# The last expert's rows by a product with gated lists, and a reordered start, in a two-layer decoder kernel

## The reference

```python
h = x                                                  # 512 tokens x 1024
h = h + gla_mixer(rms_norm(h, a_norm), w_in, w_gk2, b_gk2, o_norm, w_out)
h = h + hier_moe(rms_norm(h, m_norm[0]), ...)
k, v = split(rms_norm(h, kv_norm) @ w_kv)
h = h + stick_breaking(rms_norm(h, b_norm) @ w_q, k, v) @ w_out
h = h + hier_moe(rms_norm(h, m_norm[1]), ...)
return rms_norm(h, final_norm)

def hier_moe(t):       # top-1 of 4 groups, top-2 of its 4 experts: 2 of 16 experts per token
    combine = weights of the two chosen experts, 0 elsewhere            # 512 x 16
    for e in range(16):
        hdn = silu(t @ w_gate[e]) * (t @ w_up[e])                       # 1024 -> 512
        y += combine[:, e:e+1] * (hdn @ w_down[e])                      # 512 -> 1024
```

## Time and profile before

| | us |
|---|---|
| three runs: median (lowest, highest) | 1307.45 (1304.81, 1307.50) |
| profiled execution, whole | 1304.74 |
| its span, first to last instruction | 1303.1 |
| PE busy | 1136.8 (87%) |
| DVE busy | 819.4 (63%) |
| ACT busy | 694.4 (53%) |
| POOL busy | 157.1 (12%) |
| PE in the chain that ended last | 77% |

### The profile page before, as it was taken

How to read it: one execution, slowest core, us unless ns; L and a number is a source line. 1 busy time by engine, 2 the same in 40 slices (tenths; PEclk the granted TensorE clock), 3 DMA queues, 4 the chain that set the end, 5 groups by cost and what they waited for, 6 DMA issues and landing times.

```text
span 1303.1 us, 14486 instructions
## 1 busy us (share of the span) xinstructions
PE 1136.8 (87%) x5477; PEld 859.9 (66%) x5477; DVE 819.4 (63%) x825; ACT 694.4 (53%) x732; POOL 157.1 (12%) x169
## 2 busy tenths in 40 slices
PE   5799997974999999995799989999839999999970
PEld 4488875853677777774578867767626777777740
DVE  2454236266888888885523346662568888888846
ACT  2442433243777777775233226662427777777742
POOL 1100030012010100001100004430030010010004
PEclk9899998985999999998799988999859999999995
DMA  8343103207999999996412210003069999999925
GB/s 282 79 145 130 33 1 117 77 17 235 385 391 393 403 392 392 403 371 243 147 65 98 97 33 1 1 17 129 1 222 374 394 399 390 393 394 411 380 75 193
DMA packets 89060, 283.49 MB, mean 218 GB/s; under 512 B 11704, under 2 KB 11872, under 8 KB 89008
## 3 DMA queue, kind: packets, MB, share of 16 engines
q1 hardware_dynamic: 70272, 239.09, 48.5%
q0 software_dynamic: 11024, 39.07, 9.0%
q10 hardware_dynamic: 7712, 4.63, 1.1%
HBM read 259.96 MB, written 22.81 MB: 217 GB/s over the span
## 4 chain that ended last, share of the span: by engine, by line
PE 77%; DVE 7%; issue 5%; POOL 4%; ACT 3%; DMA 2%; ACTq 1%; POOLq 0%; DVEq 0%
PE ps L1274 23%; PE ps L1276 23%; PE ps L1275 23%; PE ps L1458 2%; PE ps L1292 1%; POOL xn_r L1829 1%; DMA xn<-output_table,pos 1%; PE ps L1419 1%; DVE h L1170 1%; PE ps L1486 1%; DVE raw L1214 1%; DVE xn_r L1218 1%; DMA pad<-normed_rows,token 1%; POOL xn_r L1824 1%; POOL pad_r L1824 1%
## 5 line engine op out<-in xcount | busy, mean ns | idle before, releaser
L816 DVE TENSOR_TENSOR w_lo<-raw,w_hi 128x2048 fp32r<-128x2048 f32 x72 | 164.7, 2289 | 94.8 <-ACT w_hi L470 94.6
L470 ACT CAST w_hi<-raw 128x2048 fp32r<-128x2048 f32 x72 | 137.7, 1912 | 117.7 <-PE ps L1276 117.5
L1274 PE MATMUL ps<-xT_hi,s_hi 128*96 128x512 f32 (+1 forms) x392 | 157.0, 400 | 8.6 <-DVE s_lo L910 5.2
L816 DVE TENSOR_TENSOR xT_lo<-raw,xT_hi 128x2048 fp32r<-128x2048 f32 x64 | 146.1, 2288 | 20.4 <-ACT xT_hi L470 20.4
L1274 PE MATMUL ps<-w_hi,s_hi 128*96 128x512 f32 x384 | 154.7, 403 | 4.6 <-DVE s_lo L992 4.6
L1276 PE MATMUL ps<-xT_hi,s_lo 128*96 128x512 f32 (+1 forms) x392 | 155.5, 397 | 0.0
L1275 PE MATMUL ps<-xT_lo,s_hi 128*96 128x512 f32 (+1 forms) x392 | 154.7, 395 | 0.0
L1276 PE MATMUL ps<-w_hi,s_lo 128*96 128x512 f32 x384 | 152.9, 398 | 0.0
L1275 PE MATMUL ps<-w_lo,s_hi 128*96 128x512 f32 x384 | 152.1, 396 | 0.0
L470 ACT CAST xT_hi<-raw 128x2048 fp32r<-128x2048 f32 x64 | 122.0, 1912 | 38.3 <-PE ps L1276 38.3
L1274 PE MATMUL ps<-w_hi,xT_hi 128*128 128x512 f32 x304 | 122.1, 401 | 12.9 <-DVE w_lo L820 6.4
(11 more groups left out here) (282 smaller groups left out, 2004.9 us busy)
## 6 DMA issues: line engine op xcount, KB each, us to landing
raw<-in_m_w_up SPq DMA_DIRECT2D x64, 1024.0 KB, 10.5
xn<-in_m_w_gate SPq DMA_DIRECT2D x60, 1024.0 KB, 11.6
raw<-in_m_w_down SPq DMA_DIRECT2D x60, 1024.0 KB, 11.2
raw<-in_a_w_in SPq DMA_DIRECT2D x12, 1024.0 KB, 5.9
output_table<-pad POOLq DMA_DIRECT2D x32, 384.0 KB, 6.4
raw<-in_w_kv SPq DMA_DIRECT2D x8, 1024.0 KB, 7.4
raw<-in_a_w_out SPq DMA_DIRECT2D x4, 1024.0 KB, 5.7
raw<-in_m_w_gate SPq DMA_DIRECT2D x4, 1024.0 KB, 8.8
```

Source lines behind the costliest of these rows:

```text
L470: se.copy(hi, raw_block).then_inc(A["hi_done"], 1)
L816: ve.tensor_tensor(lo, raw_block, hi, ALU.subtract).then_inc(V["lo_done"], 1)
L1274: te.matmul(o, a_hi, b_hi, start=start, stop=False)
```

## The change

1. **The last expert of a layer** (expert 15) is not stored; the gathers read zeros for its rows. After the router's weights DVE makes gated lists in three more instructions: it multiplies `at_row` by the weight where the chosen expert is 15 (L1172 and L1173 of the changed kernel) and adds the halves of the two choices (L1174). PE transposes them into PSUM (L1543) after expert 1's input, and DVE copies them out to `last_rows`. After the last `y_out`, PE multiplies `last_rows` with `y_sb` (L1599, float32, two instructions of 512 columns for each token tile), and DVE adds the product to `h` from PSUM (L1188). Those are three additions for each tile instead of two. The table rows of expert 15 are zeroed at the start of the program.
2. **The overflow loop** stands ahead of the last down product on every engine. POOL's eight gathers now wait only for the first 15 stores.
3. **The additions' order** is changed (`ADDS`), and in layer 0 the tiles 1 to 3 are transposed only when all additions are done. `dense_first` makes the products of tiles 2 and 3 after the first transposition. The row of token factors moves from ahead of the last tile to between its two halves.
4. **The start**: tile 0 is transposed ahead of the gains. The low-rank weight and its three companions are loaded by SP after the input tiles, and they are scaled and split ahead of `tile_lo` of tiles 1 to 3. The squares stand between the tiles' copies. Panels are renumbered, so that the first one after the gates writes other PSUM banks than the gates' and need not wait for the bias.
5. **Smaller moves**: in the linear attention the score products stand ahead of the key transposes. Ahead of the stick-breaking attention, `panel_out_features(13)` stands ahead of `split(B + 13)`. In the last norm DVE does tiles 0, 1 and 3 in one step each, and POOL and ACT only tile 2.

```diff
+        ADDS = [(0, 0), (0, 1), (1, 0), (1, 1), (2, 0), (2, 1), (0, 2), (1, 2), (3, 0), (3, 1), (2, 2), (3, 2)]
+
+        def added(layer, i, k):
+
+            return len(ADDS) * layer + ADDS.index((i, k)) + 1
+
+        def last_banks(i):
+
+            first = (0, 3072, 1024, 3072)[i]
+            return psf[:, first:first + D]
...
                     load(streams[0][1], 1)
+            with nc.allow_non_contiguous_dma(reason="512 gate biases and 16 columns a row"):
+                for dst, src in ((lr_raw[:, :, :], a_w_in[0, :, GK0:GK0 + RANK].rearrange("(k p) r -> p k r", p=P)),
+                                 (wgk2, a_w_gk2[0]), (bgk[:, :], a_b_gk2[0].rearrange("(h p) -> p h", p=P)),
+                                 (onorm, a_o_norm[0].partition_broadcast(P))):
+                    sp.dma_start(dst, src).then_inc(A["small_loaded"], 16)
...
             LN_EXP = "natural_log_exp_and_others"
             se.preload_act_table_set(LN_EXP)
+            tile_hi(0, 0)
             act.wait_ge(V["gains_out"], 1)
-            tile_hi(0, 0)
             split(0)
             split(1)
+            act.wait_ge(V["lr_scaled"], 1)
+            se.copy(lr_hi, lr_raw[:, :, :]).then_inc(A["lr_hi_done"], 1)
             for i in range(1, NT):
                 tile_hi(0, i)
-            norm_squares(0)
-            act.wait_ge(V["lr_scaled"], 1)
-            se.copy(lr_hi, lr_raw[:, :, :]).then_inc(A["lr_hi_done"], 1)
+                squares_of(0, i - 1)
+            squares_of(0, NT - 1)
+            rsqrt_first(0, NT)
...
                 step(I + NE - 1, B + LAST, 0, False)
-                if layer + 1 < LAYERS:
-                    split((layer + 1) * L_BLOCKS)
-                    split((layer + 1) * L_BLOCKS + 1)
-                act.wait_ge(M["blk_used"], B + NE * E_BLOCKS)
-                y_out(E, I + NE - 1)
...
                 over_loop(act, layer, tile)
+                if layer + 1 < LAYERS:
+                    split((layer + 1) * L_BLOCKS)
+                    split((layer + 1) * L_BLOCKS + 1)
+                act.wait_ge(M["blk_used"], B + NE * E_BLOCKS)
+                act.wait_ge(G["over_ended"], layer + 1)
+                y_out(E, I + NE - 1)
...
+            tile_lo(0, 0)
             dve.wait_ge(M["gains_tr"], 1)
             ve.tensor_copy(gainT[:, :], ps[:, 7, 0:5 * KT]).then_inc(V["gains_out"], 1)
             dve.wait_ge(V["gains_out"], 1)
-            tile_lo(0, 0)
             split(0)
             split(1)
-            for i in range(1, NT):
-                tile_lo(0, i)
             dve.wait_ge(A["small_loaded"], 16 * SMALL)
             ve.tensor_tensor(lr_raw[:, :, :], lr_raw[:, :, :], gainT[:, 0:KT].unsqueeze(2).broadcast_to([P, KT, RANK]),
                              ALU.mult).then_inc(V["lr_scaled"], 1)
+            dve.wait_ge(A["lr_hi_done"], 1)
+            ve.tensor_tensor(lr_lo, lr_raw[:, :, :], lr_hi, ALU.subtract).then_inc(V["lr_lo_done"], 1)
+            for i in range(1, NT):
+                tile_lo(0, i)
             norm_scale(0)
             diagonals()
...
                 over_loop(dve, layer, tile)
+                if layer + 1 < LAYERS:
+                    split((layer + 1) * L_BLOCKS)
+                    split((layer + 1) * L_BLOCKS + 1)
...
                 link(tt(w12[:, 1, :], w12[:, 0, :], ex, ALU.mult))
-
-            def combine(layer, first=0, last=2 * NT):
-
-                for n in range(first, last):
-                    i, k = COMBINE[n]
+                link(stt(base_k, tile_k, float(NE - 1), w12[:, :, :].rearrange("p k i -> p (k i)"), ALU.is_equal, ALU.mult))
+                link(tt(at_row, at_row, base_k.unsqueeze(2).broadcast_to([P, 2 * NT, CAP]), ALU.mult))
+                tt(at_row[:, 0:NT, :], at_row[:, 0:NT, :], at_row[:, NT:2 * NT, :], ALU.add).then_inc(V["last_ready"], 1)
...
+            def combine(layer, first, last):
+
+                for i, k in ADDS[first:last]:
                     if k == 0:
-                        dve.wait_ge(gathered[i], 32 * (layer + 1))
-                    if k:
-                        dve.wait_ge(V["combined"], 2 * NT * layer + n)
-                    ve.scalar_tensor_tensor(h[:, i, :], y_rows[n], w12[:, k, i:i + 1], h[:, i, :],
-                                            ALU.mult, ALU.add).then_inc(V["combined"], 1)
+                        dve.wait_ge(E[f"x_loaded{i}"], 16 * GATHERS * (layer + 1))
+                    else:
+                        dve.wait_ge(V["combined"], added(layer, i, k - 1))
+                    if k < 2:
+                        ins = ve.scalar_tensor_tensor(h[:, i, :], y_rows[COMBINE.index((i, k))], w12[:, k, i:i + 1], h[:, i, :],
+                                                      ALU.mult, ALU.add)
+                    else:
+                        dve.wait_ge(M["last_done"], NT * layer + i + 1)
+                        ins = ve.tensor_tensor(h[:, i, :], h[:, i, :], last_banks(i), ALU.add)
+                    ins.then_inc(V["combined"], 1)
...
             split(B + 2)
-            for i in range(NT):
-                combine(0, 2 * i, 2 * i + 2)
-                if i:
-                    tile_lo(3, i - 1)
-            tile_lo(3, NT - 1)
+            combine(0, 0, 8)
+            tile_lo(3, 0)
+            combine(0, 8, 12)
+            for i in range(1, NT):
+                tile_lo(3, i)
...
             split(B + 12)
+            panel_out_features(13, B + 11, qT1[:, 4:8, :], SD ** -0.5)
             split(B + 13)
-            panel_out_features(13, B + 11, qT1[:, 4:8, :], SD ** -0.5)
...
             experts(1)
-            combine(1, 0, 5)
+            combine(1, 0, 8)
             mean_square(4, 0, 2)
-            combine(1, 5, 6)
+            combine(1, 8, 11)
             refine(0, 2, final=1)
-            combine(1, 6, 8)
+            combine(1, 11, 12)
+            normed(2, [0, 1])
             mean_square(4, 2, NT)
             refine(2, NT, final=2)
...
                     half(j, 0)
                     if j < NT - 1:
                         transposed_tile(turn, event, j + 1)
+                    else:
+                        between_half()
                     half(j, 1)
...
-            dense_first(0, 0, 0, 0, low_rank)
+            dense_first(0, 0, 0, 0, gains_transposed, low_rank, token_factors)
             pe.wait_ge(V["lr_out"], 1)
             for i in range(GH):
                 ins = te.matmul(ps[:, 4 + i, :], wgk2[:, DK * i:DK * (i + 1)], lrT, start=True, stop=True)
             ins.then_inc(M["gates_done"], 1)
+            pe.wait_ge(A["panel_out"], 1)
+            dense(2, 2, True)
             pe.wait_ge(V["gates_in"], GH)
-            dense(1, 2, True)
-            pe.wait_ge(A["panel_out"], 1)
-            dense(2, 4, True)
+            dense(3, 4, True)
...
+            pe.wait_ge(V["k_toend"], 1)
+            pe.wait_ge(A["panel_out"], 4)
...
                 x_transposed(E, I + 1, 1, first_load)
+                pe.wait_ge(V["last_ready"], layer + 1)
+                for t in range(NT):
+                    ins = te.transpose(ps[0:CAP, 7, P * t:P * (t + 1)], at_row[:, t, :], ident[:, :])
+                ins.then_inc(M["last_tr"], 1)
...
                 h_transposed(E, i)
-                down(i, c + 6)
...
                 over_loop(pe, layer, tile)
+                down(i, c + 6)
+
+            def last_to_tokens(layer, tiles):
+
+                pe.wait_ge(V["last_out"], layer + 1)
+                pe.wait_ge(E["y_out"], NE * (layer + 1))
+                for i in tiles:
+                    if i == 3:
+                        pe.wait_ge(V["combined"], added(layer, 1, 2))
+                    for n in range(2):
+                        ins = te.matmul(last_banks(i)[:, BN * n:BN * (n + 1)], last_rows[:, P * i:P * (i + 1)],
+                                        y_sb[:, BN * n:BN * (n + 1)], start=True, stop=True)
+                    ins.then_inc(M["last_done"], 1)
...
-            dense_first(8, B, 3, 2, lambda: rstd_row_sums(2))
+            last_to_tokens(0, (0, 1))
+            dense_first(8, B, 3, 2, lambda: last_to_tokens(0, (2, 3)), lambda: None, lambda: rstd_row_sums(2))
...
             experts(1)
+            last_to_tokens(1, range(NT))
...
-                for i in range(1, NE + 1):
+                for i in range(1, NE):
                     if i + XG + 1 < NE:
                         gather_next(i + XG + 1)
                     pool.wait_ge(E["y_out"], I + i)
                     store(E, (i - 1) * CAP)
-                pool.wait_ge(E["y_stored"], 16 * (I + NE))
+                pool.wait_ge(E["y_stored"], 16 * (NE - 1) * (layer + 1))
+                pool.wait_ge(V["lo_done"], blocks_of(layer) + NE * E_BLOCKS)
+                pool.wait_ge(G["zeroed"], 16 * (MAX_OVER + 1))
                 S = O[layer]
...
             pool.wait_ge(G["gain_loaded"], 16 * 3)
-            for i in range(NT - 1):
-                wait_h(pool, 4, i)
```

(3 more changed lines are left out.)

133 lines of the change are left out of this document (63 added, 70 removed).

## The result

| us | before | changed |
|---|---|---|
| median of the runs | 1306.27 (4 runs, 1304.81 to 1307.50) | 1287.14 (4 runs, 1283.90 to 1287.73) |
| ratio, 95% interval | | 0.985 (0.983 to 0.987) |
| span of the profiled execution | 1303.1 | 1285.6 |
| granted clock, mean | 0.936 | 0.947 |

The account below looks back on a forecast made before the run. PE was taken as the bound, through its idle time and clock. Terms -14.6, 0, +3.3, -2.8, -1.9 and -5.3 sum to -21.3, from 1304.7 to 1283.4 us, said as 1284; forecast's own range 1279 to 1289, 8 in 10 for 1277 to 1292.

Parts of the forecast that it names:

- Term 1: Start of the kernel: earlier first matmul, no waits for the low-rank weight or gates' bias, fewer slow matmuls; -14.6 us.
- term 2: Linear attention: score products ahead of key transposes gain nothing, since both orders end at ACT; 0, bounds -1 to +1 us.
- the two old delays: Small loads at the start: taking turns with large weight descriptors (-14.6 us), or 16.2 us from issue to landing (-12.2).
- no wait over 1 us: Sign of being right: PE has no such wait between the first matmul, near 14.8, and 170 us.
- All at 2.4 GHz from about 19: Sign of being right: PE keeps its higher clock from about 19 us up to 170 us.
- Term 3: Router: three more DVE instructions ahead of the experts' first splits delay PE 1.65 us in each of two layers; +3.3 us.
- Term 4: End of layer 0's experts: gathers start 9.2 us sooner, most of it given back by additions and products; -2.8 us.
- six gathered additions and one from PSUM: End of layer 0's experts: these DVE additions (1.28 us each, and 1.2) bring tile 0 to 624.3 us.
- rival (a): Ends of both layers: third addition and float32 products use up the detour's gain, terms 4 and 6 are 0; 1291.5 us, chance 0.13.
- rival (d): Last down product: the loop's branch stalls PE, up to 2 us a layer; 1287.4 us, chance 0.05.
- Term 5: Ahead of the stick-breaking attention: L883 starts at the panel's end with the split behind it, 1.9 us sooner; -1.9 us.
- Term 6: End of the program: gathers 7.9 us sooner, 2.6 lost to DVE's longer chain; -5.3 us, bounds -7.9 to -1.

Follow-up runs that it names:

- experiment 3: Changed kernel with the four small loads issued by ACT behind the gains again, not by SP; median 1292.06 us, ratio 0.990 to the kernel before.
- Experiment 2: Changed kernel with DVE's three factor instructions moved from the router to behind the first expert's `x_lo`; median 1284.00 us, ratio 0.984 to the kernel before.
- experiment 4: Changed kernel with the last expert's four products and their additions ahead of the gathered rows, layer 0's split behind the additions; median 1280.12 us, ratio 0.982 to before.

## Why the prediction was right, and where it was off

The time lay 3.1 us above the 1284 said and inside the range. The places are those that were named, but the closeness is partly luck: the second series of the same kernel has a median of 1290.51, still inside 1277 to 1292 and outside the forecast's own 1279 to 1289, and the gain from the kernel before is 19.1 and 16.1 us in the two series, where 21.3 were said. Point by point:

**Term 1 (-14.6): 13.7 in the trace, 12.3 by undoing it together with term 2.** First matmul 14.77 (14.8 said); no wait for the low-rank weight, none for the gates' bias; DVE idles 3.48 us ahead of its query panel (3.3 said). The small loads had landed by 17.3 us; the estimate was 14 to 17, PE needed them at 19.8. Of the missing 0.9, 0.5 is the first slow stretch, 10 matmuls long instead of 7. (The price of a slow matmul is right, its reading isn't: 11 and 24 in 4 us don't give 0.43 and 0.23, since these counts take in what only overlaps a stretch and, in the second, eight matmuls of 128 columns. In order of time the starts lie 0.43 and 0.23 us apart.)

What the term rested on, the small loads: the prediction took the two old delays as alternatives, turns with large descriptors or an old price; in SP's queue all four landed right behind the last input tile (15.69), at 15.96, 16.16, 16.37 and 17.29; in ACT's own queue (experiment 3) at 16.68, 17.52, 20.48 and 22.06, among SP's weights at 19.23 and 22.83, though the last was issued 6.9 us sooner. By the Trainium skill (DMA: Bandwidth & Descriptors, Queues, rings and completion order) each DMA engine takes turns between queues and keeps ring order within one. The traces agree in the order of landing. The last load's 16.8 us against 5.1 from issue to landing overstate it, since in SP's queue most of the bytes ahead had moved when it was issued at 12.2. What the prediction did not see is the second half of the move's worth: the issue itself held ACT 3.97 us before the change and 4.50 in experiment 3. Now SP is held (6.25 us in the issue of another of the four loads), where only later loads stand behind it.

**Term 2 (0, -1 to +1): a step that failed.** "Both orders end at ACT" is right: the first product behind them starts when ACT's copy is there, 168.25. The clock behind it was not considered, though the text charged cold starts everywhere else. Scores first puts PE's two waits of 0.86 and 1.06 together into one of 2.16 (so the sign "no wait over 1 us" before 170 us failed too), and in four of seven traces the clock then fell, for 3.3 us in the first. In the other three it had fallen near 52 to 56 us, for 3.2 us in the second trace of the changed kernel. "All at 2.4 GHz from about 19" held in the first trace, until 169, and not in the second: with the waits taken out of the start, a kernel can still lose the clock while PE is busy with narrow products.

**Term 3 (+3.3): +1.3 and +1.3.** The instructions took 0.17, 0.96 and 0.60, as said. Some 0.4 us a layer didn't reach PE. Experiment 2 shows that the whole term could be had back.

**Term 4 (-2.8): -3.0 in the first trace, and luck in that.** Counted from the start of `y_out`, tile 0 was complete after 17.0 us (16.6 said: 624.3 less 607.68) and the dense matmuls began after 23.0 (23.7 said). But `y_out` was late by the slow down product while the gathers don't wait for it. In the second trace the same two are 19.0 and 25.6, and the stretch from `y_out` to the end of panel 13 gained 0.6 us, not 3.0. Among the eight traces with this order of additions it gained 2.0 to 3.1 in the three with the fall at 592, and 0.4 to 1.0 in the five without. The step that failed is the walk through the additions, "six gathered additions and one from PSUM" in a row: it put DVE's wait for tile 1's and tile 2's gathers at nothing, and that was 0.6 us in the first trace and 2.4 in the second. So in layer 0 rival (a) came near. "Most of this is given back" was right, and experiment 4 shows to whom: to the order of the twelve additions, with a split and two products in the way, 10.5 us together. The branch cost nothing: the wait ahead of the last down product is 1.74 us, before it was 1.73, against rival (d). The Trainium skill's rule on instruction fetch (Runtime: NRT & Kernel Launch, Instruction fetch mechanics) therefore has nothing to charge here; no stall of that kind shows at this place in any run.

**Term 5 (-1.9): -1.9,** and 1.8 when undone. **Term 6 (-5.3): -5.6.** Gathers 7.6 us sooner relative to `y_out` (7.9 said); the span ends 36.0 us behind the first gather (34.4 to 36.6 said), with the one collision: beside POOL's product DVE's L841 took 2.22 us, not 0.17.

**What the sum left out.** The clock: +3.3 at 168, +1.4 at 592, +0.5 at the start, -1.8 at 214. That is 3.4 of the 3.8 us between the 21.3 said and the 17.5 found. Why the clock fell at 592 and not in the kernel before, behind an equal wait, is not settled: of the twelve traces with this end of layer 0 it fell in four, the changed kernel's first and those of the split scores, the products first and the rounding first. All four are among the five with the new start in which it had not fallen near 52 us. In layer 1 the same product was slow once, with the rounding first. So the falls in one execution seem to hang together; that an edit which moves one fall can bring another is a reading of these few traces, and not shown. The 8 us between the two groups of runs in experiment 4 stay open too: they differ in mean clock, but only an execution of the quicker group was profiled.
